# A language-model block on one core: an expert's rows per round, 96 in place of 128

## The reference, cut to what matters

```python
def _moe(h, w_router, w_gate, w_up, w_down):
    xf = h.reshape(T, D)
    logits = jnp.einsum('td,de->te', xf, w_router, ...)
    top_logits, top_idx = lax.top_k(logits, TOP_K)          # 2 of 8
    gates = jax.nn.softmax(top_logits, axis=-1)
    ...
    xs = xf[tok_sorted]                                     # rows sorted by expert
    hid = jax.nn.silu(lax.ragged_dot(xs, w_gate, group_sizes)) * lax.ragged_dot(xs, w_up, group_sizes)
    ys = lax.ragged_dot(hid, w_down, group_sizes)
    ys = ys * gates.reshape(-1)[order][:, None]
    out = jnp.zeros_like(xf).at[tok_sorted].add(ys)
```

## Time and profile before

| What | Value |
|---|---|
| median of 3 runs | 1928.45 us (1926.85 to 1929.61) |
| span of the profiled execution | 1929.0 us |
| PE busy | 1893.1 us, 98% |
| DVE busy | 1497.7 us, 78% |
| ACT busy | 1246.1 us, 65% |
| POOL busy | 392.1 us, 20% |

### The profile page before, as it was taken

The page is one execution under the profiler, slowest core; times in us unless marked ns, Lnnn a source line. Parts: engine busy times, 40 slices in busy tenths (PEclk is TensorE's granted clock), DMA queues, the critical chain, the costliest instruction groups (busy, mean ns, idle before and its releaser), DMA issues.

```text
span 1929.0 us, 27194 instructions
## 1 busy us (share of the span) xinstructions
PE 1893.1 (98%) x9923; PEld 1609.9 (83%) x9923; DVE 1497.7 (78%) x1589; ACT 1246.1 (65%) x1478; POOL 392.1 (20%) x204
## 2 busy tenths in 40 slices
PE   8999999999999999999899999999999999999997
PEld 6788889998888999878788888888888888888886
DVE  7745366666765656696599999999999999899998
ACT  5654444445644444464388888888888888888886
POOL 5856870002824000382430000000000000000000
PEclk9999999999999999999999999999999999999999
DMA  9434556664433766534399999999999999999994
GB/s 279 155 130 131 175 186 214 215 226 153 140 123 121 224 216 214 162 118 142 131 376 394 380 395 361 392 396 354 394 353 396 397 354 395 355 395 396 356 396 186
DMA packets 251400, 524.53 MB, mean 272 GB/s; under 512 B 10008, under 2 KB 58784, under 8 KB 251184
## 3 DMA queue, kind: packets, MB, share of 16 engines
q1 hardware_dynamic: 244000, 506.36, 73.5%
q10 hardware_dynamic: 5088, 10.03, 1.4%
q0 software_dynamic: 2224, 6.96, 1.1%
HBM read 508.12 MB, written 15.20 MB: 271 GB/s over the span
## 4 chain that ended last, share of the span: by engine, by line
PE 90%; DVE 5%; ACT 2%; issue 1%; POOL 1%; DMA 0%; DVEq 0%; SPq 0%; ACTq 0%
PE bank L703 27%; PE bank L705 27%; PE bank L704 27%; PE bank L1056 2%; PE bank L1228 1%; DVE w_lo_sb L1810 1%; PE bank L777 1%; PE bank L750 1%; ACT w_hi_sb L1365 1%; PE bank L756 1%; POOL w_lo_sb L639 1%; PE bank L1109 0%; PE bank L1107 0%; PE bank L911 0%; PE bank L888 0%
## 5 line engine op out<-in xcount | busy, mean ns | idle before, releaser
L1810 DVE TENSOR_TENSOR w_lo_sb<-arena,w_hi_sb 128x1024 fp32r<-128x1024 f32 x672 | 806.9, 1223 | 74.0 <-ACT w_hi_sb L1365 48.0
L1365 ACT ACTIVATE w_hi_sb<-arena 128x1024 fp32r<-128x1024 f32 x672 | 710.5, 1062 | 164.9 <-PE bank L705 164.4
L703 PE MATMUL bank<-w_hi_sb,left_hi_sb 128*128 128x512 f32 (+1 forms) x1424 | 563.8, 396 | 7.4 <-issue 2.9
L705 PE MATMUL bank<-w_hi_sb,left_lo_sb 128*128 128x512 f32 (+1 forms) x1424 | 552.7, 388 | 0.0
L704 PE MATMUL bank<-w_lo_sb,left_hi_sb 128*128 128x512 f32 (+1 forms) x1424 | 552.2, 388 | 0.0
L1385 ACT ACTIVATE w_hi_sb<-arena 128x1024 fp32r<-128x1024 f32 (+1 forms) x269 | 280.3, 1052 | 336.2 <-PE bank L705 325.2
L639 POOL TENSOR_TENSOR w_lo_sb<-arena,w_hi_sb 128x1024 fp32r<-128x1024 f32 (+1 forms) x134 | 342.9, 2579 | 566.1 <-ACT w_hi_sb L1385 565.6
L703 PEld LDWEIGHTS bank<-w_hi_sb,left_hi_sb 128*128 128x128 f32 x1424 | 268.3, 188 | 66.2 <-issue 6.4
L705 PEld LDWEIGHTS bank<-w_hi_sb,left_lo_sb 128*128 128x128 f32 x1424 | 268.0, 188 | 56.0
L704 PEld LDWEIGHTS bank<-w_lo_sb,left_hi_sb 128*128 128x128 f32 x1424 | 268.6, 189 | 52.4 <-issue 0.7
L1822 DVE TENSOR_TENSOR w_lo_sb<-arena,w_hi_sb 128x1024 fp32r<-128x1024 f32 x135 | 163.8, 1219 | 126.4 <-ACT w_hi_sb L1385 125.5
(11 more groups left out here) (326 smaller groups left out, 1622.4 us busy)
## 6 DMA issues: line engine op xcount, KB each, us to landing
arena<-in_moe_w_gate SPq DMA_DIRECT2D x112, 1024.0 KB, 7.0
arena<-in_moe_w_up SPq DMA_DIRECT2D x112, 1024.0 KB, 8.1
arena<-in_moe_w_down SPq DMA_DIRECT2D x112, 1024.0 KB, 7.6
arena<-in_w_in SPq DMA_DIRECT2D x45, 1024.0 KB, 5.1
arena<-in_w_ffn_in SPq DMA_DIRECT2D x22, 1024.0 KB, 6.2
arena<-in_w_out SPq DMA_DIRECT2D x12, 1024.0 KB, 5.0
arena<-in_w_ffn_out SPq DMA_DIRECT2D x11, 1024.0 KB, 4.9
arena<-in_dense_w_gate SPq DMA_DIRECT2D x11, 1024.0 KB, 5.9
```

Source lines behind the costliest of these rows:

```text
L703: pe.matmul(out, still[0], moving[0], start=start, stop=False)
L705: return pe.matmul(out, still[1], moving[0], start=False, stop=stop)
L1365: act.activation(expert_buffer(w_hi_sb, j), expert_piece(j % MOE_SUBS), ACT.Copy) \
L1810: dve.tensor_tensor(expert_buffer(w_lo_sb, j), expert_piece(j % MOE_SUBS), expert_buffer(w_hi_sb, j).bitcast(F32), ALU.subtract) \
```

## The change

`CAP` is 96 in place of 128, and `MAX_ROUNDS`, the quotient of 256 tokens by `CAP` rounded up, becomes 3 in place of 2. With it, in the code that every execution runs:

- all stationary operands of the expert matmuls are 96 columns wide, their output has 96 rows; moving columns and the number of matmuls stay;
- the transposes of hidden values and of taken rows write 96 columns each; copies and splits of them handle 384 values per partition in place of 512;
- `gather` moves 96 columns in place of 128; `e_rows`, `e_y` and the DMAs of them have 96 rows;
- `sent` has 2304 rows in place of 2048; it is filled by 16 transfers of 144 rows, each read from 72 partitions, in place of 16 transfers of 128 rows read from 128 partitions;
- `count_rounds` has a second comparison and an addition.

```diff
-CAP = 128
+CAP = 96
 MAX_ROUNDS = -(-TOKENS // CAP)
...
         hid_hi, hid_lo = ([a[:, 512 * i:512 * i + 512] for i in range(2)] for a in (hid_hi_sb, hid_lo_sb))
+        e_hid_hi, e_hid_lo = ([a[:, 0:4 * CAP] for a in whole] for whole in (hid_hi, hid_lo))
...
-            pool.wait_ge(sem("rows_filled"), 16 * EXPERTS * MAX_ROUNDS)
+            pool.wait_ge(sem("rows_filled"), 16 * 2 * EXPERTS)
...
-                    hid = [tiles(a[s % 2], 4) for a in (hid_hi, hid_lo)]
+                    hid = [tiles(a[s % 2], 4) for a in (e_hid_hi, e_hid_lo)]
...
-            fill = over(const_sb[:, P:P + D // 2], 1, 2)
+            FILL_ROWS = EXPERTS * MAX_ROUNDS * CAP // (2 * EXPERTS)
+            fill = over(const_sb[0:FILL_ROWS // 2, P:P + D // 2], 1, 4)
...
-                act.dma_start(sent[number // MAX_ROUNDS, number % MAX_ROUNDS, :, :].rearrange("c (a d) -> c a d", a=2), fill) \
+                part = sent_rows[number * FILL_ROWS:(number + 1) * FILL_ROWS, :]
+                act.dma_start(part.rearrange("(c b) (a d) -> c (b a) d", b=2, a=2), fill) \
                     .then_inc(sem("rows_filled"), 16)
...
-                    act.activation(hid_hi[s % 2], misc_bank[s % 2][:, 0:4 * CAP], ACT.Copy) \
+                    act.activation(e_hid_hi[s % 2], misc_bank[s % 2][:, 0:4 * CAP], ACT.Copy) \
...
-                    dve.tensor_tensor(hid_lo[s % 2], pair_bank[2 + s % 2][:, 0:4 * CAP], hid_hi[s % 2].bitcast(F32),
+                    dve.tensor_tensor(e_hid_lo[s % 2], pair_bank[2 + s % 2][:, 0:4 * CAP], e_hid_hi[s % 2].bitcast(F32),
```

## The result

The changed kernel takes 1933.15 us (median of 11 runs, 1931.89 to 1934.77) against 1928.56 us before (11 runs, 1926.85 to 1931.02). The ratio is 1.0022, with a 95% interval of 1.0015 to 1.003. The forecast was 1911.6 us, with a range up to 1924: the time lies outside, and on the slower side of before.

What follows compares the result with a forecast made beforehand. PE's own matmul stream in the expert stage was taken as the bound. Gains of 9.1 (expert matmuls), 7.5 (transposes) and 0.2 us (copies), 16.8 in all, off the median 1928.45 gave 1911.6 us, range 1893 to 1924.

Steps and rivals of the forecast that it cites:

- What bounds the kernel: Expert stage: PE's own stream sets the end, so the distance between matmul starts counts; 119.06 us per expert.
- Expert matmuls: Expert stage: 96 stationary columns in place of 128 save 2.3 ns on 3936 matmuls, 9.1 us (0 to 27.6).
- The straight line: Expert matmuls: overhead interpolated between 13.3 ns at 128 and 6.3 ns at 32 stationary columns; 2.3 ns less, chance 0.45.
- Transposes: Turns of hidden values and taken rows: 280 transposes fall from 109 to 82.7 ns, 7.5 us gained.
- The load: Expert stage weight load: shrinks from 188 towards 161 ns, hidden under the matmul before it, worth nothing itself.
- ACT, DVE, gather, fills: Shorter copies gain 0.2 us (0 to 0.3); round count, gather and larger zero fills were counted as about nothing.
- The base of the sum: Profiled execution's span of 1929.0 us was put 0.55 us above the median 1928.45, from which gains were subtracted.
- (1) to (3): Rivals: flat overhead, 1920.7 us, chance 0.25; step at any width below 128, 1893.1 us, 0.10; no change, 1928 us, 0.12.
- (1): Rival, expert matmuls: overhead stays 13.3 ns at 96 columns, only transposes gain; 1920.7 us, chance 0.25.
- (4): Rival, expert stage: granted clock halves, 427 ns per matmul; 2735 us if all 4032 are hit; chance 0.03.
- (5): Rival, expert stage: 96-column loads lose a fast mode; at three times the load pace 2364 us; chance 0.02.
- the other terms: Gains apart from expert matmuls: transposes 7.5 us and shorter copies at the first expert's start 0.2 us.

Runs made afterwards that it cites:

- exp. 2: Changed kernel with expert matmuls loading 128 stationary columns again, hidden pieces still 96 apart: 1927.34 us against 1928.12 for the kernel before, ratio 0.9992.
- exp. 3: Kernel before the change with only the expert matmuls' stationary slices cut to 96 columns: 1938.52 us, ratio 1.0049.
- exp. 4: Changed kernel with expert loads of 128 stationary columns and hidden pieces 128 columns apart: 1922.94 us against 1928.6 for the kernel before, ratio 0.9972.
- exp. 5: Changed kernel with 88 rows per round, loads of 88 stationary columns, hidden pieces 128 columns apart: 1930.7 us, ratio 1.0014 to the kernel before.
- exp. 6: Changed kernel with 84 rows per round, loads of 128 stationary columns, hidden pieces 128 apart: 1922.31 us against 1928.6 for the kernel before, ratio 0.9967.
- experiment 1: Separate program of back-to-back matmuls at stationary widths 8 to 128 in three modes; one-pass float32, 512 moving columns: 230.0 ns at 96, 226.7 at 128.

## Why the prediction was wrong, point by point

**What bounds the kernel** was read rightly. In after and the five variants the change of the expert stage, from its first to its last matmul, gives the change of the median within 1.0 us:

| us | after | exp. 2 | exp. 3 | exp. 4 | exp. 5 | exp. 6 |
|---|---|---|---|---|---|---|
| expert stage, against before's 951.7 us | +3.9 | -1.7 | +10.4 | -6.0 | +1.5 | -6.0 |
| median, against before on the same chip | +4.6 | -0.8 | +10.4 | -5.7 | +2.1 | -6.3 |

**Expert matmuls** (9.1 us gain foretold, 0 to 27.6): this step failed, and in its sign. The straight line between 32 and 128 columns gave 2.3 ns less per matmul; it was 3.3 ns more. The term came to 11.7 us lost (9.8 from matmul to matmul, with the 1.9 us taken out that the transposes gave behind the turns, below). Some 1.0 us of it is the 96-column spacing of the hidden pieces, which the prediction gave no price at all. Two things were wrong in the line. It took the earlier trace rows, at 256 moving columns, as two points of a smooth law for 512, where 32 columns are slower than 128 (231.7 against 226.7 ns); even at 256 moving, 64 columns (113.3 ns) lie below both 32 (117.8) and 128 (119.8). Nor is the point at 32 columns a fixed one: the distances behind the earlier trace rows are 113.3 ns each (the rounded rows gave 112.9), and the same width and moving columns alone run at 117.8. And its bounds left out a loss without a reason that excludes one: "nothing" was taken as the floor, though the rows held no width between 32 and 128. The step that should have warned stood there: 13.3 ns over the moving columns, not explained by anything in the trace. Who doesn't know what a number is made of can't know which way it moves.

**The Trainium skill's rule**, "TensorE: Matmul & The Clock Gate", Back-to-back issue gap: the moving columns over 2.4 GHz and about 2.5 ns, with no stationary width in it. The page gives it for a matmul by itself, which the prediction left out. In experiment 1, where every matmul has a load of its own, it holds in plain float32 (three widths) and bf16 (five), with 215.8 ns. For a stream of loads and matmuls the same section has about 131 ns at 512 columns, and no row here is near that. In the one-pass float32 mode the rule doesn't hold: there it is 13.3 to 22.2 ns over 512 columns, and it depends on the width. By the rule after would have taken 1920.7 us; the runs reach 1922.3 to 1922.9 only where loads are 128 columns wide and begin at a multiple of 64.

**Transposes** (7.5 us): right. The distances between them fell to 82 ns as foretold, which is 217 distances and 5.6 us. The other 63 transposes are the last of each group, and in after they gave 1.9 us in the distance behind the next matmul, together 7.5. But that part hung on a condition that the prediction didn't see: it comes only with the narrower load (experiment 4 has the shorter transposes and gets 5.6 us), just as the narrower load alone gives nothing (experiment 3).

**The load**: near 161 ns foretold, 161 measured. It was worth nothing in itself, as foretold.

**ACT, DVE, gather, fills**: PE's wait for the multiply shrank by 0.4 us over the stretch in place of growing by some hundredths per expert; PE came later itself. The gather took 5.64 us against 5.99, with 0.64 of the clock against 0.52, so the two can't be compared. No transfer and no split was late in the stage. The stage began 1.8 us earlier, outside the half microsecond that the prediction allowed. In the five other variants it begins between 960.2 and 962.2 us; the kernel before, at 963.35, is the latest. In the first 57 us, where PE waits for the first loads, it was busy 48.50 us before and 50.28 in after. So it looks like a matter of that one execution; that isn't shown, since before has one profile. The stage accounts for 3.9 of the 4.6 us in the median; 0.7 us stay open.

**The base of the sum.** The profiled execution of after has a span of 1931.1 us and a time of 1932.93: 1.8 us lie around the span. If they do before as well, the execution with a span of 1929.0 us took 1930.8, near the longest of its 11 runs (1931.02), and not 0.55 us above the median.

**The rivals.** None of the five was it. (1) to (3) held the pace at or below 226.7; the reason that (1) gave, an array switched as a whole, stands on no run. (4) didn't come: the clock is 1.00 in the stage. (5) named a slower side by the load, which was 161 ns and never the bound between matmuls. The rival that was missing is "the pace at 96 columns is worse than at 128", from 2.0 ns on: 3936 x 1.96 ns eat the 7.7 us of the other terms.

## What to carry to other kernels

Where matmuls with 512 moving columns run back to back in the one-pass float32 mode, give them stationary operands of the full 128 columns that start at a multiple of 64 columns, even if fewer carry data, and moving operands that do so too. What fewer rows save, save elsewhere (here in the transposes, 5.6 us). This is no rule for other lengths: with 256 moving columns 128 was the slowest of the widths in experiment 1 (119.8 ns, against 113.3 at 64), and with 384 the width made no difference. A distance between starts that exceeds its moving columns by something unexplained isn't to be interpolated: measure it at the very width, and behind the same neighbours. When an operand shrinks, ask also which load is the last to arrive behind each group of short matmuls: two costs can cover each other there, and taking away one shows nothing.

## What the runs showed of the hardware that was not expected

In the one-pass float32 mode at the full clock (2.4 GHz) the start distance of matmuls with 512 moving columns is one of several fixed rhythms, 226.7 to 235.5 ns, chosen by width, by first column and, at 88 columns, by what runs just ahead. 128 columns from a multiple of 64 always reached 226.7, after up to some ten matmuls. Plain float32 and bf16 (both 215.8 ns) show no such thing, nor does the half clock (426.7 ns, at 128 columns in experiment 1 and at 88 in experiment 5). Why there are several rhythms no run here isolates; it stays open.

Weight loads by form in the first experiment, mean ns in the column before the last:

```profile
L55 PEld LDWEIGHTS bank<-move_r,still_r 128*128 128x128 f32 x240 | 42.5, 194 | 15.8 <-ACT move_b L43 9.5
...
L55 PEld LDWEIGHTS bank<-move_r,still_r 128*96 128x96 f32 x144 | 21.1, 161 | 4.0
...
L55 PEld LDWEIGHTS bank<-move_b,still_b 128*112 128x112 bf16 x48 | 6.2, 130 | 4.1
...
L55 PEld LDWEIGHTS bank<-move_b,still_b 128*128 128x128 bf16 x48 | 4.7, 98 | 5.6
```

Of the 240 loads in the first row 48 are of the stretch that begins at the half clock; the other 192 take 188 ns. In bf16 the load of 128 columns is shorter than that of 112. In the one-pass float32 mode it is 188 ns at 128 and 187 at 127, in a line with the narrower ones. The Trainium skill, "TensorE: Matmul & The Clock Gate", Weight-path perf modes, gives a fast weight load for exactly 128 stationary columns and a type other than float32. The bf16 rows agree with it, and the one-pass mode behaves like float32 (190 ns at 128, 163 at 96), so 96 columns had no such mode to lose. What they lost was the rhythm.
